# A hybrid decoder layer on one core: the first five column units taken on x without the norm's root

## The reference

```python
def rmsnorm(x, g):
    y = x * lax.rsqrt(jnp.mean(x * x, axis=-1, keepdims=True) + RMS_EPS)
    return y * g

n = rmsnorm(x, norm1)                       # 288 tokens x 2048
c_rw, c_att, c_gate = _split(n @ w_in, ...) # 27 + 21 + 32 tiles of 128 columns
o_rw  = rwkv7_mix(c_rw, ...)                # recurrence of 16 heads
o_att = attend(rope(q), rope(k), v, rope(qi), rope(ki), wi)   # top-k, then attention
merged = sigmoid(g_rw) * (o_rw @ p_rw) + sigmoid(g_att) * (o_att @ p_att)
h = x + merged @ w_o
y = rmsnorm(h + conv_glu(rmsnorm(h, norm2), ...), norm_f)
```

## Time and profile before

| what | value |
|---|---|
| time, median of 3 runs | 1869.41 us (1866.0 to 1872.04) |
| the profiled execution's own time | 1866.89 us |
| its span, first to last instruction | 1865.3 us |
| PE busy | 1819.5 us, 98% of the span |
| DVE, ACT, POOL busy | 1124.7, 727.5, 61.7 us |
| mean granted clock of PE | 0.99 |

### The profile page before, as it was taken

How to read it: one execution, slowest core, us unless ns; L and a number is a source line. 1 busy time by engine, 2 the same in 40 slices (tenths; PEclk the granted TensorE clock), 3 DMA queues, 4 the chain that set the end, 5 groups by cost and what they waited for, 6 DMA issues and landing times.

```text
span 1865.3 us, 41090 instructions
## 1 busy us (share of the span) xinstructions
PE 1819.5 (98%) x16700; PEld 1737.9 (93%) x16700; DVE 1124.7 (60%) x1962; ACT 727.5 (39%) x1014; POOL 61.7 (3%) x102
## 2 busy tenths in 40 slices
PE   4999999999999999999999999999999999999997
PEld 3999888888888888899999999999999999999997
DVE  5454585556777777776556666666666666443444
ACT  3333343454444444443344333333333333333332
POOL 2600000000000000000000000000000000000000
PEclk7999999999999999999999999999999999999998
DMA  4644333432223333364446444444454454544453
GB/s 173 215 159 158 128 136 119 153 126 93 103 103 102 104 106 106 104 217 173 161 165 215 169 163 159 166 170 157 161 177 157 157 173 161 203 166 164 160 170 128
DMA packets 50832, 283.59 MB, mean 152 GB/s; under 512 B 7104, under 2 KB 12288, under 8 KB 24656
## 3 DMA queue, kind: packets, MB, share of 16 engines
q1 hardware_dynamic: 43488, 260.87, 41.1%
q10 hardware_dynamic: 3216, 12.82, 1.8%
q0 software_dynamic: 4064, 8.98, 1.5%
HBM read 274.38 MB, written 8.27 MB: 152 GB/s over the span
## 4 chain that ended last, share of the span: by engine, by line
PE 94%; DVE 4%; ACT 1%; DMA 0%; issue 0%; ACTq 0%; DVEq 0%; SPq 0%
PE bank L584 29%; PE bank L586 27%; PE bank L585 27%; PE bank L903 1%; PE bank L938 1%; DVE w_lo L533 1%; DVE x_raw L1630 1%; PE bank L565 1%; PE bank L601 0%; PE bank L1003 0%; PE bank L925 0%; PE bank L680 0%; ACT w_hi L549 0%; PE bank L770 0%; DVE max L1706 0%; PE bank L754 0%
## 5 line engine op out<-in xcount | busy, mean ns | idle before, releaser
L584 PE MATMUL bank<-x_split,w_lo 128*128 128x288 f32 x2944 | 900.8, 306 | 20.4 <-DVE x_split L1636 16.7
L585 PE MATMUL bank<-x_split,w_hi 128*128 128x288 f32 x2944 | 870.7, 296 | 0.0
L586 PE MATMUL bank<-x_split,w_hi 128*128 128x288 f32 x2944 | 868.3, 295 | 0.0
L549 ACT ACTIVATE w_hi<-w_raw 128x2048 fp32r<-128x2048 f32 (+1 forms) x264 | 472.5, 1790 | 577.2 <-PE bank L586 563.0
L533 DVE TENSOR_TENSOR w_lo<-w_raw,w_hi 128x2048 fp32r<-128x2048 f32 (+1 forms) x238 | 503.7, 2116 | 316.3 <-ACT w_hi L549 316.1
L584 PEld LDWEIGHTS bank<-x_split,w_lo 128*128 128x128 f32 x2944 | 554.1, 188 | 45.1 <-issue 26.1
L585 PEld LDWEIGHTS bank<-x_split,w_hi 128*128 128x128 f32 x2944 | 555.4, 189 | 3.1 <-issue 0.7
L586 PEld LDWEIGHTS bank<-x_split,w_hi 128*128 128x128 f32 x2944 | 556.5, 189 | 0.0
L584 PE MATMUL bank<-act_split,w_lo 128*128 128x288 f32 x704 | 208.6, 296 | 0.0
L585 PE MATMUL bank<-act_split,w_hi 128*128 128x288 f32 x704 | 207.7, 295 | 0.0
L586 PE MATMUL bank<-act_split,w_hi 128*128 128x288 f32 x704 | 207.0, 294 | 0.0
(11 more groups left out here) (374 smaller groups left out, 1499.5 us busy)
## 6 DMA issues: line engine op xcount, KB each, us to landing
w_raw<-in_w_up SPq DMA_DIRECT2D x88, 1024.0 KB, 4.8
w_raw<-in_w_in SPq DMA_DIRECT2D x48, 1024.0 KB, 4.9
w_raw<-in_w_down SPq DMA_DIRECT2D x64, 704.0 KB, 4.1
w_raw<-in_w_gate SPq DMA_DIRECT2D x32, 1024.0 KB, 4.9
w_raw<-in_w_p SPq DMA_DIRECT2D x16, 1024.0 KB, 4.9
w_raw<-in_w_o SPq DMA_DIRECT2D x16, 1024.0 KB, 4.8
x_raw<-in_x SPq DMA_DIRECT2D x4, 576.0 KB, 6.5
h<-in_x ACTq DMA_DIRECT2D x1, 2304.0 KB, 10.3
```

Source lines behind the costliest of these rows:

```text
L549: actv(WHI[:, slot, 0:kt], WRAW[:, slot, 0:kt], ACT.Copy).then_inc(sem("w_hi"), 1)
L584: mm(out, wl, hi, start=first and k == ks[0], stop=False, skip_group_check=True)
L585: mm(out, w, lo, start=False, stop=False, skip_group_check=True)
L586: ins = mm(out, w, hi, start=False, stop=last and k == ks[-1], skip_group_check=True)
```

## The change

**Start.** x is split without `rstd`: ACT makes the high part of x times the gains (`first_hi`), DVE the low part (`first_lo`), before the norm is known. The first five units (`SWAP` = 4) are multiplied with this, and DVE evacuates them with a multiplication by `rstd` (`scaled_out`) in place of ACT's copy. Meanwhile DVE scales x by gains and `rstd` (`normed`) behind the low splits of units 2 and 3, and the normed high and low parts (`norm_hi`, `norm_lo`) replace the first ones quarter by quarter, as unit 4 has done with a quarter (`x_used`); the last quarter comes after unit 4. From unit 5 all is as before. The squares go in quarters into a buffer of their own, DVE folds the last eight tiles into two, and PE sums ten tiles (eight ahead of unit 0, two within it). The matrix of 1/2048 is set by DVE and no longer loaded. The weights of units 0 and 1 are split in four parts each by ACT and DVE, none by GpSimd. The gains are loaded ahead of x, the constants behind unit 1's weights, GpSimd's cache loads start after unit 2.

**Columns.** The index weights move from unit 2 to unit 6; the ropes are spread over units 7 to 23, up to two in a unit; the last rope goes ahead of the low split of unit 25.

**Attention.** `FILL_TOPK` goes from 58 to 40, with 14 blocks more (`FILL_SAMPLE`) behind the first step's scores, which wait for the sample's own selection alone (`bias_s_ready`). `FILL_SOFTMAX` goes from 9 to 14, `FILL_P_T` from 10 to 5. DVE's `streamed(FILL_P_T)` moves ahead of its wait for the exponentials. Ahead of the lora products there are 22 blocks (14 and 8), and ACT's `filled` and DVE's `streamed` for them stand before and behind the lora's `mix`.

```diff
@@ constants @@
-FILL_MIX, FILL_FIRST, FILL_DECAY, FILL_BONUS = 20, 6, 4, 14
-FILL_OUT, FILL_ROPE, FILL_REQUESTS, FILL_TOPK_S, FILL_DOTS, FILL_TOPK = 3, 7, 2, 24, 3, 58
-FILL_SCORES, FILL_SOFTMAX, FILL_P_T, FILL_PV = 8, 9, 10, 4
+FILL_MIX, FILL_LORA, FILL_FIRST, FILL_DECAY, FILL_BONUS = 14, 8, 6, 4, 14
+FILL_OUT, FILL_ROPE, FILL_REQUESTS, FILL_TOPK_S, FILL_DOTS, FILL_TOPK, FILL_SAMPLE = 3, 7, 2, 24, 3, 40, 14
+FILL_SCORES, FILL_SOFTMAX, FILL_P_T, FILL_PV = 8, 14, 5, 4
@@ PE @@
-            pe.wait_ge(sem("main_c_in"), 16)
-            for t in range(KT):
-                norm_sum(0, t, t % 2, SQ)
+            pe.wait_ge(sem("x_split"), 1)
+            first_sums(range(0, 4), 3)
+            first_sums(range(4, 8), 6)
...
+                    if n < 2:
+                        if q < 3:
+                            pe.wait_ge(sem("w_part"), 3 * n + q + 1)
+                        else:
+                            pe.wait_ge(sem("w_split"), n + 1)
+                    if n in (0, SWAP + 1):
+                        pe.wait_ge(sem("x_split"), (4 if n else 0) + q + 1)
+                    ins = blocks(n, n % 2, range(4 * q, 4 * q + 4), BK[n % 2][:, 0:N], XN, q == 0, q == 3)
+                    if n == SWAP and q < 3:
+                        ins.then_inc(sem("x_used"), 1)
+                    if q == 3:
+                        ins.then_inc(sem("unit_done"), 1)
+                    if n == 0 and q == 2:
+                        first_sums((8, 9), KT).then_inc(sem("norm_sq_used"), KT)
@@ ACT @@
+            first_hi(0)
+            first_hi(1)
+            first_squares(0)
+            first_hi(2)
+            first_squares(1)
+            first_hi(3)
+            first_weights(0)
+            first_squares(2)
+            first_squares(3)
+            first_weights(1)
@@ DVE @@
-            norm(0, RSTD, XRAW, XRAW, True)
-            dve.wait_ge(sem("x_split"), 4)
+            for i in range(4):
+                first_lo(i)
+            first_weights(0)
+            dve.wait_ge(sem("norm_sq"), 12)
+            st.done(V.tensor_tensor(SQ[:, 8:12, :], SQ[:, 8:12, :], SQ[:, 12:16, :], ALU.add))
+            V.tensor_tensor(SQ[:, 8:10, :], SQ[:, 8:10, :], SQ[:, 10:12, :], ALU.add).then_inc(sem("norm_sq"), 4)
+            first_weights(1)
+            norm_rstd(0, RSTD)
...
             for n in range(FIRST_COLS):
-                split_lo(dve, n + 2, n % 2)
+                if n <= SWAP:
+                    scaled_out(n)
+                if n == SWAP:
+                    norm_lo(3)
+                if n < FIRST_COLS - 1:
+                    split_lo(dve, n + 2, n % 2)
+                if n < 2:
+                    normed(2 * n)
+                    normed(2 * n + 1)
+                if n == SWAP - 1:
+                    for i in range(3):
+                        norm_lo(i)
...
@@ DVE, an attention step of the prompt @@
+                streamed(FILL_P_T + (FILL_PV if n == 1 else 0))
                 dve.wait_ge(sem("exp"), n + 1)
...
-                streamed(FILL_P_T)
@@ ACT and DVE, the lora @@
+            filled(FILL_MIX)
             act.wait_ge(sem("lora_mix"), 1)
...
             mix(COLS[:, T_LW:T_LG + 1, :], RKV, LMU).then_inc(sem("lora_mix"), 1)
+            streamed(FILL_P_T + FILL_PV + FILL_MIX)
             dve.wait_ge(sem("lora_act"), 1)
```

More of the change, by code:

```diff
@@ L177 @@
 ROPE_TILES = [T_Q + i for i in range(8)] + [T_K, T_K + 1] + [T_QI + i for i in range(8)] + [T_KI]
+SWAP = 4
+FIRST_ROPE = 7
+ROPES_BY_UNIT = {}
+for _i, _t in enumerate(ROPE_TILES[:-1]):
+    _n = max(_t - 24 + 1, FIRST_ROPE)
+    while len(ROPES_BY_UNIT.setdefault(_n, [])) == 2:
+        _n += 1
+    ROPES_BY_UNIT[_n].append(_i)
 ATT_STEPS = [("sample", 0), (0, 0), (0, 1), (1, 0), (1, 1), ("sample", 1)]
@@ L285, in build @@
     XRAW = m("x_raw", [P, KT, N])
-    SQ = m("squares", [P, 2, N])
-    RSTD = m("rstd", [P, N])
+    squares_at = m.at
+    SQ = m("squares", [P, KT, N])
+    RSTD = region(squares_at)("rstd", [P, N])
     m = region(big)
@@ L560, in settle, with first_sums @@
                 eng.sem_inc(sem("pe_step"), 1)
[L562 to L566, removed]
+            def first_sums(tiles, squared):
+                pe.wait_ge(sem("norm_sq"), squared)
+                for t in tiles:
+                    ins = mm(BK[2][:, 0:N], mean_ones, SQ[:, t, :], start=t == 0, stop=True, skip_group_check=True)
+                return ins
             def last_sum(k, total, squares):
@@ L1275, in sample_values @@
                 ins.then_inc(sem("v_new"), 1)
+            filled(FILL_TOPK)
+            sample_values(0, 0)
+            filled(FILL_SAMPLE)
+            act.wait_ge(sem("v_t"), 1)
+            act.wait_ge(sem("bias_ready"), 1)
+            actv(VTOK[:].rearrange("p k f -> p (k f)"), BK[4][:], ACT.Copy).then_inc(sem("v_tok"), 1)
             for n, (kind, which) in enumerate(ATT_STEPS):
                 if kind == "sample":
-                    sample_values(n, which)
+                    if which:
+                        sample_values(n, which)
                     act.wait_ge(sem("s_max"), n + 1)
@@ new lines, in normed, with norm_lo @@
+            def normed(i):
+                for t in range(4 * i, 4 * i + 4):
+                    ins = V.scalar_tensor_tensor(XRAW[:, t, :], XRAW[:, t, :], NORMS[:, 0, t:t + 1], RSTD[:],
+                                                 ALU.mult, ALU.mult)
+                ins.then_inc(sem("normed"), 1)
+            def norm_lo(i):
+                q = slice(4 * i, 4 * i + 4)
+                dve.wait_ge(sem("x_hi"), 4 + i + 1)
+                V.tensor_tensor(XN[:, 1, q, :], XRAW[:, q, :], XN[:, 0, q, :].bitcast(F32),
+                                ALU.subtract).then_inc(sem("x_split"), 1)
@@ L1655, in rope, with group_queries @@
+            def group_queries(half):
+                for g in range(KVH):
+                    for b in range(4):
+                        c0 = SEQ + DS * (4 * half + b)
+                        ins = V.tensor_copy(QZ[:, g, b, 4 * g:4 * g + 4, :], COLS[:, T_Q + 4 * g:T_Q + 4 * g + 4, c0:c0 + DS])
+                ins.then_inc(sem("q_grouped"), 1)
             def rope(i):
```

206 lines of the change are left out of this document (109 added, 97 removed).

## The result

The changed kernel takes 1846.66 us in the median of 4 runs (1845.74 to 1847.54), the kernel before, beside it, 1869.13 (1866.0 to 1872.04). The ratio is 0.9885 with a 95% interval of 0.9873 to 0.9897: faster, by 22.5 us of the median, where 1843 and 26 were forecast. Of the profiled executions, this one took 1846.31 in all and the one of before 1866.89, which is 20.6 apart; the working of the prediction is held against these 20.6.

What follows compares the result with a forecast made beforehand. PE was taken as the bound, busy 1819.5 of 1865.3 us, leaving 46 us of waiting, low-clock stretches and its own work. Head -21.7 and middle -4.3 gave -26.0, so 1843 us, range 1835 to 1851.

Steps and rivals of the forecast that it cites:

- The head: Start of the kernel through unit 0: unit 0 ends at 25.3 against 47.0, worth -21.7 us.
- the middle: Last rope, top-k, attention and lora together: -4.3 us, with bounds of -10.4 and 0.
- (a): Last rope, now ahead of a low split on DVE: its wait of 1.7 goes, -1.7 us.
- (b): Top-k: bias wait of 3.54 and slow clock behind it go (-5.3), new 2.0 wait at unit 32: -3.3 us.
- (c): Attention: 1.5 of low-part waits removed, +1.0 for less cover of the transposed probabilities over six steps: -0.5 us.
- (d): Ahead of the lora's products: unit 44's low split behind DVE's mix, a wait of 3.1 for 1.9: +1.2 us.
- high parts until 7.6: Step at the start: ACT makes the high part of x's first quarter, landed at 5.7, until 7.6 us.
- the clock of 0.53: Top-k: granted clock of 0.53 from 288.4 to 292.0, half of 3.6, was to go with the bias wait.
- the bound of zero: Bound for the middle's total: 0 if the attention term costs 3 and the lower clock follows unit 32's 2.0 wait.
- The middle pays in full: Rival: new waits at units 32 and 44 don't come, -32 us in all, 1837; chance 0.14.
- Unit 0 is slow: Rival: unit 0 at the lower clock and DVE just late in units 2 to 6, -18 us, 1851; chance 0.18.
- the two about DVE's backlog and GpSimd's cache issues: Rivals: DVE's backlog gives back the head's gain, no change, 0.03; GpSimd's cache issues block DVE, slower, near 1880, 0.03.

Runs made afterwards that it cites:

- the early load: Changed kernel with a 1-element Copy on ACT ahead of the waits for gains and x, so the table load runs earlier: 1845.08 us, ratio 0.9873.
- 38 blocks: Changed kernel with FILL_TOPK 38 and FILL_SAMPLE 16 in place of 40 and 14: 1842.57 us, ratio 0.9866 to the kernel before.
- the four edits: Changed kernel with early table load, unit 24's evacuation ahead of output transfers, FILL_TOPK 38 with FILL_SAMPLE 16, unit 44's split before the mix: 1835.39 us.
- the new head alone: Changed start and columns, with the fillers and order of the kernel before from the top-k to the lora: 1842.26 us, ratio 0.9868.

## Why the prediction was right, and where it was off

Its range held the time, and faster was right. The head carried it; the middle, forecast at -4.3, came out at nothing. By its terms, in the profiled executions (starts of the same instruction in both, less 0.40 for each block of filler that one has done more):

| term | forecast | in the profiles |
|---|---|---|
| head, to unit 23's end | -21.7 | -20.8 |
| (a) last rope | -1.7 | -0.7 |
| (b) top-k | -3.3 | -1.1 |
| (c) attention | -0.5 | +0.6 |
| (d) lora | +1.2 | +1.2 |
| sum, and own time | -26.0 | -20.8, and -20.6 |

**The head.** Nearly every step came as told: full clock in unit 0, unit 0's evacuation behind `rstd` and done at 28.57 (forecast 29.0), unit 2's split at 30.77 (31.2), no wait in units 1 to 6, scalings at 0.44. It failed in one small step, "high parts until 7.6": ACT's table load of 1.28 stands behind the wait for x. In the kernel before it ran at 1.92; there ACT's first function waits for x alone, here for the gains and x, which is likely why, but wasn't tested by itself. The experiment with the early load gives 1.25 of it back. Shorter steps on ACT (0.44 a copy, 1.05 from one square to the next instruction) won 0.6 of it back by unit 0's start. Of the head's 21 us, 9 are GpSimd out of DVE's way. The other 12 are what is left for all the rest of the new start: the root out of the chain above all, as `rstd` is ready only after unit 0's end, and in it 2.0 for the full clock in unit 0, which the sums ahead of it bring. The prediction named these and did not divide them; no run defers the root and nothing else, so the 12 are a remainder.

**(b) was mis-sized in its clock.** "With it the clock of 0.53" took 1.8 off, and the new wait of 2.0 at unit 32 (measured: 2.24) was priced without one. It brought a fall of the same length, so nothing of the 1.8 came. That was not bound to happen, but likely: over the seven profiles with this wait the falls cost 1.5 on average, and the bound of zero had the case in it ("the lower clock follows the 2.0"). With 38 blocks both go.

**(a).** The rope's wait went, but unit 26's low part is 1.19 late where it was 0.33. It hangs on ACT, where three transfers stand ahead of unit 24's evacuation, and one of their issues took 1.45, where it had taken 0.62. In seven later profiles with that code the issue took 0.89 to 1.18 and the wait is 0.63 to 0.90, so 0.3 to 0.6 of the miss stays and the rest is chance. Why this issue takes longer behind the new columns is open; with unit 24's evacuation ahead of it (the four edits) the wait is gone.

**(c)** went as told in kind: the wait of 1.46 in the fourth prompt step fell to 0.29 (1.2 gained for the 1.5 forecast), one of 0.83 for the transposed probabilities came, and 0.9 is spread over gaps too short to be listed. 1.0 was set for the cost, 1.7 came. The 0.83 stands in the second of the six steps, where the counts had the third, and what made it was not in the term: ACT's copy is behind a high split as forecast, but the split itself waited for its weights (timeline, engine ACT).

```profile
298.24 1.92 ACT L560 ACTIVATE w_hi<-w_raw 128x2048 fp32r<-128x2048 f32 x1 [2.74 <-DMA w_raw<-in_w_in]
300.07 0.57 ACT L1352 ACTIVATE prob_t<-bank 128x512 f32<-128x512 f32 x1
```

**(d)** was right to 0.1 in its wait: 3.17 for 3.1. A fall of 3.4 us followed it, as one had followed the 1.87 before.

**The rivals.** "The middle pays in full" is refuted: the waits at units 32 and 44 came in every profile with this code, at 2.2 and 3.2. "Unit 0 is slow" and the two about DVE's backlog and GpSimd's cache issues are refuted by the head's 20.8; DVE's splits beside those issues take 2.28 and 2.29. What the middle is worth stays open within the noise: -1.1 by itself, and some +3 as the difference of the changed kernel to the one with the new head alone, which the intervals can't tell from nothing.

## What to carry to other kernels

A factor that is constant along the contraction can be taken out of the product and put into the evacuation; here the new start, of which that is the core, turned 12 us of a serial chain into work beside PE. Before moving arithmetic, look for DVE and GpSimd instructions with SBUF inputs that overlap: 9 us were only that. Whoever trades one wait of PE for another of 2 us has won little, because the clock can fall behind either; place the filler so that PE's next need lies behind something it can do, as 38 blocks do and 40 don't.

## What the runs showed of the hardware

Between unit 0 and the end of PE's work, the granted clock fell to half for either 3.4 us or 6.8 us (from the windows of 1 us), 1.7 or 3.4 us lost. Every such fall began during a wait of PE or within 2.0 us of its end. The two waits for x at the start of the kernel before apart, there were nine waits of 3.16 us and more, one in each of nine profiles: all nine had a fall. Of eighteen between 1.69 and 2.74 us, ten had one. The shorter ones had none. The same wait in the same program went both ways: 2.24 in the changed kernel with a fall, 2.23 in its second profile without. The Trainium skill ("TensorE: Matmul & The Clock Gate", "What's actually happening") says that the number of slow matmuls at a kernel's start varies from run to run of the same kernel; these traces show the like for the falls within one.

The two versions with no wait of PE above 1.02 us once unit 0 has begun have runs within 1.6 and 2.4 us of each other, the kernel before within 5 to 8 over its four sets. That the falls are what spreads the medians is likely but not shown: the changed kernel, with waits of 2.2 and 3.2, has sets within 1.8 and 4.4.
